# Experts' blocks of 96 rows for one expert and 32 rows for it or for a small guest expert

## The chip, the core and the metric

The kernel runs on one core of a Trainium2 chip. The metric is the device time of one execution in microseconds (us). The engines are TensorE (PE; its weight loads are listed apart as PEld), VectorE (DVE), ScalarE (ACT), GpSimd (POOL) and SyncE (SP).

## The reference

Two transformer blocks run one after the other over 512 tokens of width 1024, all in float32. The change lies in the end of the second one, a mixture of experts:

```
scores = sigmoid(h @ router_w); choice = scores + router_bias      # 512 x 64
# the 4 best of 8 groups of experts, in them the 8 best experts of each token
gw = scores of the 8, divided by their sum, times 2.5
y = sum over a token's 8 experts of gw * (silu(h @ gate_e) * (h @ up_e)) @ down_e
shared = (silu(h @ sh_gate) * (h @ sh_up)) @ sh_down
x = x + g2 * (y + shared)
out = rms_norm(x) * final_g
```

An expert's gate and up weights are 1024 x 256 each, its down weights 256 x 1024. There are 512 x 8 = 4096 pairs of token and expert. How many of them an expert gets is known only on the chip, from the router.

## The kernel before

The program is a list of phases. Each is a block in which every engine has its own instruction list, and semaphores order the lists. Three phases are touched.

**phase_route** computes the router's choice, then a plan. DVE runs a chain of small dependent steps (`step`, each waits for the one before). The plan cuts each expert's tokens into blocks of up to 128 rows, deals the blocks over lanes, and finds each token's slot. PE meanwhile computes the shared expert in the order of its list: `gate_up(0..3)`, counts and ranks, its down product, then `list_products`, which turns slots into lists of tokens. ACT copies the shared expert's result to `K.shared`.

**phase_experts** runs N trips. A trip has three steps s = 0, 1, 2 (UNROLL), each a block of 128 rows. Steps 0 and 1 use lanes 0 and 1, whose weights serve all 128 rows. Step 2 is split in halves of 64 rows, lanes 2 and 3, each with an expert and weights of its own (`halves`). N is the number of trips that holds all full blocks in lanes 0 and 1 and all halves. For each block

- POOL gathers the tokens' rows (`gather`) and loads the lane's weights (`load`), both by indirect DMA. A gate and up set is 2 MB and a down set 1 MB. A lane's weights are skipped where its expert is that of the trip before. Waiting for the buffers' last reader orders the loads: there is one buffer per lane, and it may be filled again when that lane's products of the trip before are done.
- DVE transposes the rows in 16 instructions (`move_x`).
- PE computes gate and up into a PSUM bank: 8 slices of the width, in each one `matmul` of the 128 tokens (or two of 64) against 512 columns. Then it computes the block before's down product (`down_products`, 4 pairs of slice and half), and two transposes of this block's product.
- ACT and DVE compute silu, the product and the copies out, and SP writes 512 KB to `expert_out`.

A float32 `matmul` instruction appears in the trace as two weight loads and two matmul records. In PE's rows a form like 128*64 is the shape of the weights, rows by columns of the array, and a tile of 64 columns writes 64 partitions of PSUM.

**phase_combine** gathers each token's 8 rows, sums 3 of them on DVE (on top of `K.shared`) and 5 on PE, and applies the gate, the residual and the last norm.

Of the kernel before, what the change touches and what calls it, by code (L numbers as in the profile page):

```python
# [13 lines left out]
P = 128  # L14
D = 1024
KD = D // P
T = 512
# [2439 lines left out]
LANES, LANE = 4, 32  # L2457
NOWHERE = 1.0e6
RC_LOWER, RC_TOKEN, RC_LANE, RC_TRIP, RC_ROW, RC_TWOS, RC_EXPERT, RC_COUNT, RC_N = 0, 64, 68, 69, 70, 71, 103, 167, 295


def phase_route(nc, K, ctx):
    d, sb, sig = K.dram, K.buffer, K.flag
    w_r, bias, const, tri = K.route_in
    K.shared = sb("shared", [P, NT, D])
# [4 lines left out]
    K.source = sb("lane_sources", [P, LANES * LANE]).bitcast(U32)  # L2470
    sc, tmp = (sb(n, [P, NT, EXPERTS]) for n in ("r_score", "r_tmp"))
    eq = sb("r_eq", [P, TOP, EXPERTS])
# [4 lines left out]
    full, fend, half, hend, hat, base, jump, got, got2 = (sb(f"r_{n}", [P, EXPERTS]) for n in ("full", "fend", "half", "hend", "hat", "base", "jump", "got", "got2"))  # L2477
    few, few_end, many = (sb(f"r_{n}", [P, EXPERTS]) for n in ("few", "few_end", "many"))
    ones = sb("r_ones", [P, EXPERTS])
    trips, num = sb("r_trips", [P, 2, LANE]), sb("r_num", [P, 24])  # L2480
    diag, again, src_f = sb("r_diag", [P, P]), sb("r_again", [P, P]), sb("r_src", [P, P])
# [9 lines left out]
    selected, cnt_mm, eb_done, eb_t = (sig(n) for n in ("selected", "counts_summed", "block_experts", "block_experts_turned"))  # L2491
    slots_done, hot, list_mm = sig("slots_ready"), sig("slot_digits_ready"), sig("lists_summed")
    gu_mm, sg_act, sh_mul, dn_mm, sh_out = (sig(n) for n in ("shared_gu", "shared_silu", "shared_product", "shared_down", "shared_out"))
    grp = lambda ap: ap.rearrange("p t (g e) -> p (t g) e", e=EXPERTS // GROUPS)
# [3 lines left out]
    with nc.Block() as block:  # L2498
        @block.sync
        def _(sp):  # L2500
            pass

        @block.tensor
        def _(pe):
# [20 lines left out]
            gate_up(2)  # L2525
            gate_up(3)
            pe.wait_ge(eb_done.sem, 1)
            eb_t.by(pe.matmul(K.bank[3][:, 0:P], K.ones[:, :], diag[:, :], start=True, stop=True))
            free(K, gu_mm)

            w = take(K, pe)[:, 0:2 * D].rearrange("p (k n) -> p k n", k=2)
# [20 lines left out]
        @block.scalar  # L2552
        def _(act):
            expo.by(act.activation(sc[:, :, :], K.psum[:, :].rearrange("p (t n) -> p t n", t=NT)[:, :, 0:EXPERTS], ACT.Exp, scale=-1.0))
            for m in range(2):
                act.wait_ge(gu_mm.sem, m + 1)
                sg_act.by(act.activation(hg[:, m, :], K.bank[4 + m], ACT.Silu))
            for n in range(2 * NT):
                t, half = divmod(n, 2)
                act.wait_ge(dn_mm.sem, n + 1)  # L2560
                sh_out.by(act.activation(K.shared[:, t, 512 * half:512 * half + 512], K.bank[6 + n % 2], ACT.Copy))

        @block.gpsimd
        def _(pool):
            pass

        @block.vector
        def _(dve):
# [47 lines left out]
            N, N2, F, F4, S = (num[:, m:m + 1] for m in range(5))  # L2616
            step(ts(full[:, :], cnt, BLOCK // 2 + 0.5, None, ALU.is_gt))
            step(ts(half[:, :], cnt, 0.5, None, ALU.is_gt))
            for k in range(1, T // BLOCK):
                step(stt(out=full[:, :], in0=cnt, scalar=BLOCK * k + BLOCK // 2 + 0.5, in1=full[:, :], op0=ALU.is_gt, op1=ALU.add))  # L2620
                step(stt(out=half[:, :], in0=cnt, scalar=BLOCK * k + 0.5, in1=half[:, :], op0=ALU.is_gt, op1=ALU.add))
            scan(fend, full)
            scan(hend, half)
            step(ts(trips[:, 0, :], const[:, RC_TWOS:RC_TWOS + LANE], fend[:, last:], None, ALU.is_lt))
            step(ts(num[:, 5:6], hend[:, last:], 0.5, None, ALU.mult))
            step(ts(trips[:, 1, :], const[:, RC_TWOS:RC_TWOS + LANE], num[:, 5:6], None, ALU.is_lt))
            step(tt(trips[:, 0, :], trips[:, 0, :], trips[:, 1, :], ALU.max))
            step(dve.tensor_reduce(N, trips[:, 0, :], AX.X, ALU.add))
            step(ts(N2, N, 2.0, None, ALU.mult))

            step(tt(half[:, :], half[:, :], full[:, :], ALU.subtract))
            step(stt(out=few[:, :], in0=full[:, :], scalar=0.5, in1=half[:, :], op0=ALU.is_lt, op1=ALU.mult))
            step(tt(many[:, :], half[:, :], few[:, :], ALU.subtract))
            scan(few_end, few)
            scan(hend, many)
            step(stt(out=hat[:, :], in0=hend[:, :], scalar=few_end[:, last:], in1=many[:, :], op0=ALU.add, op1=ALU.subtract))
            step(stt(out=got[:, :], in0=hat[:, :], scalar=N2, in1=many[:, :], op0=ALU.is_ge, op1=ALU.mult))
            step(tt(full[:, :], full[:, :], got[:, :], ALU.add))
            step(tt(many[:, :], many[:, :], got[:, :], ALU.subtract))
            scan(fend, full)  # L2640
            step(tt(hat[:, :], hat[:, :], many[:, :], ALU.mult))
            step(tt(few_end[:, :], few_end[:, :], few[:, :], ALU.subtract))
            step(tt(few_end[:, :], few_end[:, :], few[:, :], ALU.mult))
            step(tt(hat[:, :], hat[:, :], few_end[:, :], ALU.add))
            step(tt(half[:, :], few[:, :], many[:, :], ALU.add))
            step(stt(out=num[:, 6:7], in0=N, scalar=-4.0, in1=fend[:, last:], op0=ALU.mult, op1=ALU.add))
            step(ts(got[:, :], hat[:, :], N2, num[:, 6:7], ALU.is_ge, ALU.mult))
            step(stt(out=hat[:, :], in0=hat[:, :], scalar=N2, in1=got[:, :], op0=ALU.add, op1=ALU.add))
            step(tt(base[:, :], fend[:, :], full[:, :], ALU.subtract))
            step(stt(out=jump[:, :], in0=hat[:, :], scalar=1.0, in1=fend[:, :], op0=ALU.mult, op1=ALU.subtract))  # L2650
            step(tt(jump[:, :], jump[:, :], half[:, :], ALU.mult))

            V = num[:, 7:8]
            step(ts(num[:, 8:9], const[:, RC_TRIP:RC_TRIP + 1], N, NOWHERE, ALU.is_ge, ALU.mult))
            step(ts(V, const[:, RC_LANE:RC_LANE + 1], N, const[:, RC_TRIP:RC_TRIP + 1], ALU.mult, ALU.add))
            step(tt(V, V, num[:, 8:9], ALU.add))
            step(ts(got[:, :], base[:, :], V, None, ALU.is_le))
            step(stt(out=got[:, :], in0=fend[:, :], scalar=V, in1=got[:, :], op0=ALU.is_gt, op1=ALU.mult))
            step(stt(out=got2[:, :], in0=hat[:, :], scalar=V, in1=half[:, :], op0=ALU.is_equal, op1=ALU.mult))
            step(tt(got[:, :], got[:, :], got2[:, :], ALU.add))  # L2660
# [3 lines left out]
            link(dve, ts(diag[:, :], K.ident[:, :], num[:, 9:10], None, ALU.mult), eb_done)  # L2664

# [535 lines left out]
```

## Time and profile before

| what | us |
|---|---|
| median of 3 runs (2342.84 to 2349.06) | 2344.48 |
| span of the profiled execution, which is also its time | 2343.3 |
| phase_route (1606 to 1666) | 60.0 |
| phase_experts until PE's first product (1666 to 1681.7) | 15.7 |
| PE's first to last product of phase_experts (1681.7 to 2265.2) | 583.5 |
| rest, phase_combine (2265.2 to 2343.3) | 78.1 |

The span counts from the first to the last instruction. The last rows of the table add up to the stretch from 1606 us on. What comes ahead of that is the same program before and after.

### The profile page before, as it was taken

The numbers are of one execution on the slowest core, as the hardware profiler recorded it, in microseconds if no ns is written. First come the engines' busy times: TensorE is split into PE (matmuls) and PEld (weight loads), VectorE is DVE, ScalarE is ACT, GpSimd is POOL, SyncE is SP. The second block draws the span as 40 slices with busy tenths as digits, with TensorE's granted clock in tenths as the row PEclk, the third lists the DMA queues.
The fourth block names the chain that finished last, engine by engine and source line by source line (L and its number), as shares of the span: only waits on it lengthen the run. The fifth ranks groups of instructions, "written<-read, shape, count | busy, mean of one in ns | idle before, by whom it ended". The sixth has DMA issues, their size and how long they took to land. (4 is left out here: it accounts for less than half of the span.)

```text
span 2343.3 us, 27600 instructions
## 1 busy us (share of the span) xinstructions
PE 2151.4 (92%) x10395; PEld 1246.3 (53%) x10395; DVE 1330.6 (57%) x2524; ACT 461.2 (20%) x916; POOL 396.7 (17%) x771
## 2 busy tenths in 40 slices
PE   6999989999999999999879999998699999999975
PEld 3444554777785458883443788445333333333322
DVE  3448863766672134434968333535766766767745
ACT  2013561121120011004235232011011111111111
POOL 0005000111000000000000000000444444444433
PEclk9999999999999999999989999998799999999988
DMA  9422000535524015981111100401499999898976
GB/s 389 180 81 81 36 1 20 233 144 216 215 81 179 36 72 229 391 306 54 37 57 58 51 3 4 177 36 54 180 372 397 425 353 421 344 407 357 413 281 252
DMA packets 68999, 446.60 MB, mean 191 GB/s; under 512 B 12276, under 2 KB 12932, under 8 KB 44066
## 3 DMA queue, kind: packets, MB, share of 16 engines
q0 software_dynamic: 36176, 254.42, 27.1%
q1 hardware_dynamic: 32722, 190.78, 21.0%
q8 instruction: 71, 1.16, 0.2%
q14 instruction: 30, 0.24, 0.0%
HBM read 416.27 MB, written 73.45 MB: 209 GB/s over the span
## 5 line engine op out<-in xcount | busy, mean ns | idle before, releaser
L965 PE MATMUL psum<-arena 128*128 128x256 f32 x1904 | 416.7, 381 | 2.1 <-PEq L1005 2.0
L2824 PE MATMUL psum<-arena 128*64 128x512 f32 (+1 forms) x1088 | 366.1, 600 | 38.9 <-DVE arena L2872 16.6
L965 PEld LDWEIGHTS psum<-arena 128*128 128x128 f32 x1904 | 361.4, 190 | 62.6 <-issue 14.0
L2872 DVE STREAM_TRANSPOSE arena<-arena 32x256 f32<-32x256 f32 x832 | 362.1, 435 | 15.8 <-DMA arena<-scratch_h,arena 4.1
L2824 PEld LDWEIGHTS psum<-arena 128*64 128x64 f32 (+1 forms) x1088 | 143.8, 165 | 226.6 <-issue 197.7
L2815 PE MATMUL psum<-arena 128*64 128x512 f32 (+1 forms) x544 | 186.2, 598 | 1.2 <-ACT arena L2850 1.2
L1067 PE MATMUL psum<-arena 128*128 128x512 f32 x352 | 151.8, 592 | 0.3 <-PEq L1091 0.3
L2815 PEld LDWEIGHTS psum<-arena 128*64 128x64 f32 (+1 forms) x544 | 68.5, 163 | 113.2 <-issue 111.8
L869 PE MATMUL psum<-arena 128*128 128x512 f32 x256 | 111.2, 593 | 2.3 <-DVE arena L2432 1.5
L1067 PEld LDWEIGHTS psum<-arena 128*128 128x128 f32 x352 | 66.6, 190 | 83.4 <-issue 83.4
L2878 DVE COPY arena<-psum 128x512 f32<-128x512 f32 x51 | 35.3, 692 | 132.7 <-PE psum L2815 132.7
L420 DVE SCALAR_TENSOR_TENSOR arena<-arena 128x512 f32<-128x512 f32 x120 | 94.8, 833 | 5.8 <-PEq L456 4.5
L2846 ACT ACTIVATE arena<-psum 128x256 f32<-128x256 f32 x51 | 19.6, 384 | 378.2 <-PE psum L2824 371.0
L869 PEld LDWEIGHTS psum<-arena 128*128 128x128 f32 x256 | 48.1, 190 | 61.2 <-issue 58.9
L1200 DVE SCALAR_TENSOR_TENSOR arena<-arena 128x511 f32<-128x511 f32 x88 | 69.3, 788 | 16.0 <-ACT arena L1164 13.6
L1164 ACT ACTIVATE arena<-arena 128x512 f32<-128x512 f32 x44 | 33.5, 807 | 215.9 <-DVE arena L984 215.9
L2922 POOL DMA_INDIRECT arena<-in_exp_down,arena x68 | 69.3, 1018 | 34.2 <-issue 34.2
L2922 POOL DMA_INDIRECT arena<-in_exp_gu,arena x68 | 69.2, 1017 | 32.8 <-issue 32.8
L1600 PE MATMUL psum<-arena 128*128 128x512 f32 x128 | 63.9, 628 | 10.8 <-ACT arena L1700 8.8
L972 DVE TENSOR_TENSOR arena<-arena,psum 128x512 f32<-128x512 f32 x34 | 23.3, 687 | 88.8 <-PE psum L965 88.8
L244 PE MATMUL psum<-arena 128*32 128x512 f32 x384 | 49.6, 637 | 25.6 <-DMA arena<-in_w_ada 25.6
L1352 DVE TENSOR_TENSOR arena<-psum,arena 128x1024 f32<-128x1024 f32 x4 | 4.9, 1225 | 115.7 <-PE psum L1067 115.7
(521 smaller groups left out, 2932.0 us busy)
## 6 DMA issues: line engine op xcount, KB each, us to landing
scratch_expert_out<-arena SPq DMA_DIRECT2D x18, 2048.0 KB, 19.9
scratch_expert_out<-arena SPq DMA_DIRECT2D x51, 512.0 KB, 9.9
arena<-in_w_ada SPq DMA_DIRECT2D x12, 2048.0 KB, 16.8
arena<-in_ada_w POOLq DMA_DIRECT2D x12, 2048.0 KB, 8.8
arena<-in_w_up SPq DMA_DIRECT2D x22, 1024.0 KB, 4.8
arena<-in_w_in SPq DMA_DIRECT2D x9, 2048.0 KB, 11.0
arena<-in_w_down SPq DMA_DIRECT2D x5, 2048.0 KB, 8.6
arena<-in_w_o SPq DMA_DIRECT2D x2, 2048.0 KB, 8.4
```

The lines of the kernel that those rows point to most:

```text
L244: last = pe.matmul(bank[32 * j:32 * j + 32, :], vec[:, k, :], w[:, 512 * k:512 * k + 512], start=(r == 0), stop=(r == 1))
L420: K.tap.by(dve.scalar_tensor_tensor(out=conv[:, k, :], in0=x, scalar=w, in1=conv[:, k, :], op0=ALU.mult, op1=ALU.add))
L869: last = pe.matmul(K.bank[2 * t + half], lhs[:, k, P * t:P * t + P], row(k)[:, 512 * half:512 * half + 512], start=(k == 0), stop=(k == pe ...
L965: last = pe.matmul(out, w[:, k, :], x[:, k, :], start=(k == 0), stop=(k == KH - 1))
L1067: out = pe.matmul(K.bank[2 * t + half], K.hmid[:, k, P * t:P * t + P], w[:, k % 4, 512 * half:512 * half + 512], start=(first and k == inn ...
L1200: link(dve, dve.scalar_tensor_tensor(out=c[:, to], in0=u[:, fr], scalar=taps[:, n, 4 * half + tap:4 * half + tap + 1], in1=c[:, to], op0=A ...
L1600: last = pe.matmul(K.bank[6 if m == 0 else 7], K.gw[:, m % 2, P * k:P * k + P], K.h[:, k, :], start=(k == 0), stop=(k == KD - 1))
L2815: last = pe.matmul(K.bank[5 + half][r, :], ht[:, b, P * k + r.start:P * k + r.stop], down[:, lane, D * k + 512 * half:D * k + 512 * half + ...
L2824: last = pe.matmul(K.bank[2 + s][r, :], xt[:, s, P * k + r.start:P * k + r.stop], gu[:, lane, 2 * E_FF * k:2 * E_FF * (k + 1)], start=(k = ...
L2872: last = dve.transpose(channels[c:c + 32, :, a:a + 32], tokens[a:a + 32, :, c:c + 32])
L2878: dve.tensor_copy(out[:, (s - 1) % U, 512:D], K.bank[6]).then_inc(out_dve.sem, 1)
L2922: pool.indirect_dma_start(to[:, lane, :], None, src, offset, bounds_check=EXPERTS * P - 1, oob_is_err=False).then_inc(landed_[lane].sem, 16)
```

## The change

The 128 rows of a block become 96 rows of the lane's expert and 32 rows (partitions 0 to 31) that belong to it or to a guest. All three lanes are alike. Each has two weight buffers, OWN and VISITOR. An expert with at most 32 tokens (`tiny`) is a guest in a block whose 32 rows its host does not need (`spare`). A guest that finds no room becomes a host (`alone`). N is now a third of the number of hosts' blocks. The plan, the slots and the lists follow. `K.table` holds for each block which buffer its 32 rows use, and PE reads it (`choice`).

PE's product over 128 rows is issued in three parts, `rows_of`: rows 32 to 63 and rows 64 to 127 with OWN, then rows 0 to 31 with the buffer picked by a register. The loop's buffers change too: the weights take 2 x 3 sets instead of 4, `e_h` is gone (the product is written over `g`), `ht` has one buffer, and the third buffer of gathered rows shares memory with the router's scores. It is cleared and filled only when DVE's last use of them (`weigh_step`) is done.

In phase_route the shared expert's down weights are multiplied by the gate row on POOL, and POOL adds the shared expert's result to the residual `K.res` there. phase_combine starts its sum with a multiplication instead.

```
+            def choice(i, s):
+                return pe.value_load(table[0:1, at(i, s)], min_val=OWN, max_val=VISITOR)
+            def rows_of(bank, left, weights, lane_pick, col, first, last_):
+                for r in (slice(GUEST, 2 * GUEST), slice(2 * GUEST, P)):
+                    pe.matmul(bank[r, :], left[:, r], weights[:, OWN, col:col + 512], start=first, stop=last_)
+                picked = weights[:, bass.ds(lane_pick, 1), col:col + 512].rearrange("p a n -> p (a n)")
+                return pe.matmul(bank[0:GUEST, :], left[:, 0:GUEST], picked, start=first, stop=last_)
...
                 for half in range(2):
                     for k in range(2):
-                        for r, lane in halves(b):
-                            last = pe.matmul(K.bank[5 + half][r, :], ht[:, b, P * k + r.start:P * k + r.stop],
-                                             down[:, lane, D * k + 512 * half:D * k + 512 * half + 512], start=(k == 0), stop=(k == 1))
+                        last = rows_of(K.bank[5 + half], ht[:, P * k:P * k + P], down[b], pick, D * k + 512 * half, k == 0, k == 1)
...
             def step(i, s):
+                if s == 0:
+                    if not (isinstance(i, int) and i == 0):
+                        picks[U - 1] = choice(i, -1)
+                    picks[0] = choice(i, 0)
                 blocks_done(pe, turned, i, s, 0)
-                landed(pe, gu_in, i, s, 0)
+                landed(pe, gu_in, i, s, 0, 32)
                 for k in range(KD):
-                    for r, lane in halves(s):
-                        last = pe.matmul(K.bank[2 + s][r, :], xt[:, s, P * k + r.start:P * k + r.stop],
-                                         gu[:, lane, 2 * E_FF * k:2 * E_FF * (k + 1)], start=(k == 0), stop=(k == KD - 1))
+                    last = rows_of(K.bank[2 + s], xt[:, s, P * k:P * k + P], gu[s], picks[s], 2 * E_FF * k, k == 0, k == KD - 1)
                 last.then_inc(gu_mm.sem, 1)
                 if not (isinstance(i, int) and i + s == 0):
-                    down_products(i, s)
+                    down_products(i, s, picks[(s - 1) % U])
+                if s < U - 1:
+                    picks[s + 1] = choice(i, s + 1)
...
-                for _, lane in halves(s):
-                    offset = bass.IndirectOffsetOnAxis(ap=wrows[:, index + lane:index + lane + 1], axis=0)
-                    pool.indirect_dma_start(to[:, lane, :], None, src, offset, bounds_check=EXPERTS * P - 1, oob_is_err=False).then_inc(landed_[lane].sem, 16)
+                for who in (OWN, VISITOR):
+                    offset = bass.IndirectOffsetOnAxis(ap=wrows[:, index + 2 * s + who:index + 2 * s + who + 1], axis=0)
+                    pool.indirect_dma_start(to[s][:, who, :], None, src, offset, bounds_check=EXPERTS * P - 1, oob_is_err=False).then_inc(landed_[s].sem, 16)
...
-            link(pool, pool.memset(xg[:, :, :], 0.0), cleared)
+            link(pool, pool.memset(xg2[:, :, :], 0.0), cleared)
...
+                    if isinstance(i, int) and i == 0 and s == 1:
+                        pool.wait_ge(weigh_step.sem, 3 * NT)
+                        link(pool, pool.memset(xg[U - 1], 0.0), cleared)
```

Of the plan in phase_route (`parts` counts an expert's blocks, `own` those of them that need their 32 rows themselves):

```
+            step(stt(out=tiny[:, :], in0=cnt, scalar=GUEST + 0.5, in1=parts[:, :], op0=ALU.is_lt, op1=ALU.mult))
...
+            step(tt(host[:, :], parts[:, :], tiny[:, :], ALU.subtract))
...
+            step(tt(spare[:, :], host[:, :], own[:, :], ALU.subtract))
...
+            step(ts(trips[:, :], const[:, RC_THREES:RC_THREES + LANE], host_end[:, last:], None, ALU.is_lt))
+            step(dve.tensor_reduce(N, trips[:, :], AX.X, ALU.add))
...
+            for k in range(2):
+                gated.by(pool.tensor_tensor(shared_down[:, k, :], shared_down[:, k, :], gate_row[:, :], ALU.mult))
+            for t in range(NT):
+                pool.wait_ge(sh_out.sem, 2 * t + 2)
+                added.by(pool.tensor_tensor(K.res[:, t, :], K.res[:, t, :], shared[:, t, :], ALU.add))
```

**Where instructions move.** On PE, in the body of the loop, before: from step 0's down product to step 1's. L2824 is gate and up, L2815 down (here of the split lane, in 64-row parts), L2831 the transposes; the shape is that of the output.

```order
L2815 MATMUL psum<-arena 64x512 x8
L2831 MATMUL psum<-arena 128x128 x2
L2778 REGISTER_ALU
L2824 MATMUL psum<-arena 128x512 x8
L2815 MATMUL psum<-arena 128x512 x4
```

The same engine and place in the changed kernel, from the loop's first product on; L2834 and L2836 are the two kinds of line in `rows_of`, and this pattern of four rows stands 12 times in a block (8 in gate and up, 4 in down).

```order
L2811 ISA
L2820 ISA
L2834 MATMUL psum<-arena 32x512
L2834 MATMUL psum<-arena 64x512
L2836 ISA
L2836 MATMUL psum<-arena 32x512
L2834 MATMUL psum<-arena 32x512
L2834 MATMUL psum<-arena 64x512
```

Each instruction over 128 output rows has become three, of 32, 64 and 32 rows in that order, with a register instruction ahead of the third. On PE in the changed kernel, at the end of a block, between the down product and the transposes (L2868); L2830 reads the table for the next block.

```order
L2836 ISA
L2836 MATMUL psum<-arena 32x512
L2830 ISA
L2830 TENSOR_LOAD arena
L2830 ISA x2
L2868 MATMUL psum<-arena 128x128 x2
L2811 REGISTER_ALU
```

A read from memory into PE's registers now stands in each block. On POOL, in the loop's body, one step of lane 1 before (L2908 gathers rows, L2922 loads weights):

```order
L2908 DMA arena<-scratch_h,arena 128x1024
L2913 TENSOR_TENSOR arena<-arena 128x1
L2916 ISA
L2916 COPY arena<-arena 128x1
L2918 REGISTER_ALU
L2919 TENSOR_TENSOR arena<-arena 128x1
L2922 DMA arena<-in_exp_gu,arena 128x4096
L2913 TENSOR_TENSOR arena<-arena 128x1
L2916 COPY arena<-arena 128x1
L2919 TENSOR_TENSOR arena<-arena 128x1
L2922 DMA arena<-in_exp_down,arena 128x2048
```

The same step in the changed kernel (L2944 gathers, L2956 loads):

```order
L2944 DMA arena<-scratch_h,arena 128x1024
L2949 TENSOR_TENSOR arena<-arena 128x1
L2951 ISA
L2951 COPY arena<-arena 128x1
L2951 ISA
L2951 COPY arena<-arena 128x1
L2952 REGISTER_ALU
L2953 TENSOR_TENSOR arena<-arena 128x1
L2956 DMA arena<-in_exp_gu,arena 128x4096 x2
L2949 TENSOR_TENSOR arena<-arena 128x1
L2951 COPY arena<-arena 128x1 x2
L2953 TENSOR_TENSOR arena<-arena 128x1
```

Two loads of each kind are issued for every block, where lanes 0 and 1 issued one.

## Rows read from the trace of the kernel before

**Rows 1.** The page's part 1: busy us, share of the span, instructions.

```profile
PE 2151.4 (92%) x10395; PEld 1246.3 (53%) x10395; DVE 1330.6 (57%) x2524; ACT 461.2 (20%) x916; POOL 396.7 (17%) x771
```

**Rows 2.** Windows by stage: length, engines' busy us (count), granted clock, DMA share, GB/s.

```profile
core 0: us, PE busy (x) PEld busy (x) DVE busy (x) ACT busy (x) POOL busy (x), PEclk, DMA share, GB/s
...
1681.70:2265.20 583.50, 556.78 (x1734) 224.61 (x1734) 411.12 (x923) 63.52 (x152) 260.21 (x612) 0.99 0.94 381
2265.20:2343.30 78.10, 36.69 (x81) 15.43 (x80) 36.93 (x37) 13.62 (x37) 32.64 (x32) 0.78 0.66 262
...
1666.00:1681.70 15.70, 0.01 (x1) 0.01 (x1) 11.14 (x23) 0.00 (x0) 11.92 (x22) 0.63 0.54 202
```

**Rows 3.** Groups by form, 1700 to 2240 us: gate and up, whole and split.

```profile
L2824 PE MATMUL psum<-arena 128*128 128x512 f32 x510 | 226.0, 596 | 9.8 <-DMA arena<-in_exp_gu,arena 9.8
L2824 PE MATMUL psum<-arena 128*64 128x512 f32 x512 | 113.4, 595 | 12.6 <-issue 12.6
```

**Rows 4.** Window of one whole block of lane 0, PE: busy (count), clock, DMA, GB/s.

```profile
1867.08:1877.60 10.52, 10.52 (x28) 1.00 1.03 435
```

**Rows 5.** The transposes, by source line: min/median/max ns, first and last start.

```profile
L2831 PE MATMUL psum<-arena x102: 272/273/477, 1694.6 to 2260.1; 128*128 128x128 f32 x102
```

**Rows 6.** Timeline of PE's weight loads into, along and out of a split lane's products.

```profile
start us, us, engine line op out<-in xcount [idle before <-releaser]
...
1862.27 0.19 PEld L2824 LDWEIGHTS psum<-arena 128*128 128x128 f32 x1 [0.24 <-issue]
1863.22 0.20 PEld L2815 LDWEIGHTS psum<-arena 128*64 128x64 f32 x4 [0.76 <-issue]
1863.70 0.14 PEld L2815 LDWEIGHTS psum<-arena 128*64 128x64 f32 x2 [0.29 <-issue]
1864.13 0.14 PEld L2815 LDWEIGHTS psum<-arena 128*64 128x64 f32 x2 [0.29 <-issue]
...
1865.85 0.14 PEld L2815 LDWEIGHTS psum<-arena 128*64 128x64 f32 x2 [0.28 <-issue]
1866.81 0.20 PEld L2831 LDWEIGHTS psum<-arena 128*128 128x128 f32 x2 [0.81 <-issue]
1866.97 0.30 PEld L2824 LDWEIGHTS psum<-arena 128*128 128x128 f32 x2
```

**Rows 7.** Timeline of PE in an earlier phase, where three forms follow each other.

```profile
1128.43 0.61 PE L1630 MATMUL psum<-arena 128*128 128x128 f32 x4
1128.96 0.44 PE L1643 MATMUL psum<-arena 128*64 128x128 f32 x4
1129.33 0.49 PE L1618 MATMUL psum<-arena 64*128 64x256 f32 x2
```

**Rows 8.** Timeline of PE's weight loads, four tiles of 32 columns, first phase.

```profile
21.91 0.16 PEld L244 LDWEIGHTS psum<-arena 128*32 128x32 f32 x8 [2.90 <-DMA arena<-in_w_ada]
22.36 0.13 PEld L244 LDWEIGHTS psum<-arena 128*32 128x32 f32 x4 [0.30 <-issue]
22.79 0.13 PEld L244 LDWEIGHTS psum<-arena 128*32 128x32 f32 x4 [0.30 <-issue]
```

**Rows 9.** DMA, 1681.7 to 2265.2 us: all packets, and the indirect DMAs' queue.

```profile
DMA packets 33896, 222.39 MB, mean 381 GB/s; under 512 B 8841, under 2 KB 8841, under 8 KB 19264
...
q0 software_dynamic: 26691, 196.10, 82.7%
```

**Rows 10.** Reads of the table into registers, by source line: min/median/max ns.

```profile
L2762 PEldq TENSOR_LOAD <-arena x1: 487/487/487, 1666.1 to 1666.1; - x1
...
L2762 PEldq FUSED_REGOPS  x1: 175/175/175, 1666.6 to 1666.6; - x1
```

**Rows 11.** Timeline of DVE in the plan: two of its dependent steps.

```profile
1624.46 0.23 DVE L2620 SCALAR_TENSOR_TENSOR arena<-psum,arena 128x64 f32<-128x64 f32 x1
1624.72 0.22 DVE L2621 SCALAR_TENSOR_TENSOR arena<-psum,arena 128x64 f32<-128x64 f32 x1
```

**Rows 12.** POOL's groups by form: a sum of 128x1024, and the clearing in phase_experts.

```profile
L1270 POOL TENSOR_TENSOR arena<-arena 128x1024 f32<-128x1024 f32 x4 | 9.5, 2374 | 46.0 <-PE psum L965 46.0
...
L2928 POOL MEMSET arena<- 128x3072 f32 x1 | 2.7, 2657 | 199.6 <-POOLq L2498 199.6
```

**Rows 13.** What PE waited for, 1665 to 2270 us: us in total, times, longest.

```profile
PE psum L2824 <- DMA arena<-in_exp_gu,arena: 9.8, 10, 1.5
```

More of the change, by code:

```diff
@@ L2500, in _ @@
         def _(sp):
-            pass
+            gate_in.by(sp.dma_start(gate_row[:, :], d["mod_rows"][3].partition_broadcast(P)), 16)
         @block.tensor
@@ L2615, in _ @@
             last = EXPERTS - 1
-            N, N2, F, F4, S = (num[:, m:m + 1] for m in range(5))
-            step(ts(full[:, :], cnt, BLOCK // 2 + 0.5, None, ALU.is_gt))
-            step(ts(half[:, :], cnt, 0.5, None, ALU.is_gt))
+            N, F, G, V, AFTER, FREE, TURN, TURN1 = (num[:, m:m + 1] for m in (0, 1, 2, 7, 8, 15, 16, 17))
+            step(ts(parts[:, :], cnt, 0.5, None, ALU.is_gt))
             for k in range(1, T // BLOCK):
-                step(stt(out=full[:, :], in0=cnt, scalar=BLOCK * k + BLOCK // 2 + 0.5, in1=full[:, :], op0=ALU.is_gt, op1=ALU.add))
-                step(stt(out=half[:, :], in0=cnt, scalar=BLOCK * k + 0.5, in1=half[:, :], op0=ALU.is_gt, op1=ALU.add))
@@ L2622, in _ @@
[L2622 to L2651, printed above, removed]
@@ new lines, in _ @@
+            step(ts(own[:, :], got[:, :], 0.5, None, ALU.is_gt))
+            for k in range(1, T // BLOCK):
+                step(stt(out=own[:, :], in0=got[:, :], scalar=GUEST * k + 0.5, in1=own[:, :], op0=ALU.is_gt, op1=ALU.add))
+            step(tt(spare[:, :], host[:, :], own[:, :], ALU.subtract))
+            step(dve.tensor_reduce(F, spare[:, :], AX.X, ALU.add))
+            step(ts(F, F, -0.5, 1.0, ALU.mult, ALU.add))
+            step(stt(out=F, in0=tiny_end[:, last:], scalar=0.5, in1=F, op0=ALU.mult, op1=ALU.add))
@@ new lines, in _ @@
+            step(stt(out=alone[:, :], in0=tiny_end[:, :], scalar=F, in1=tiny[:, :], op0=ALU.is_lt, op1=ALU.mult))
+            step(tt(guest[:, :], tiny[:, :], alone[:, :], ALU.subtract))
+            step(tt(host[:, :], host[:, :], alone[:, :], ALU.add))
+            scan(host_end, host)
+            step(tt(base[:, :], host_end[:, :], host[:, :], ALU.subtract))
+            step(tt(start[:, :], base[:, :], own[:, :], ALU.add))
+            step(ts(trips[:, :], const[:, RC_THREES:RC_THREES + LANE], host_end[:, last:], None, ALU.is_lt))
@@ L2659, in _ @@
-            step(stt(out=got2[:, :], in0=hat[:, :], scalar=V, in1=half[:, :], op0=ALU.is_equal, op1=ALU.mult))
-            step(tt(got[:, :], got[:, :], got2[:, :], ALU.add))
+            step(stt(out=got[:, :], in0=host_end[:, :], scalar=V, in1=got[:, :], op0=ALU.is_gt, op1=ALU.mult))
+            step(stt(out=got2[:, :], in0=start[:, :], scalar=V, in1=got[:, :], op0=ALU.is_le, op1=ALU.mult))
+            link(dve, dve.tensor_reduce(FREE, got2[:, :], AX.X, ALU.add), spare_done)
             step(tt(got[:, :], got[:, :], const[:, RC_EXPERT:RC_EXPERT + EXPERTS], ALU.mult))
@@ L2740, in phase_experts @@
     U = UNROLL
[L2741 to L2744 removed]
+    OWN, VISITOR = 0, 1
+    gu, down = [], []
+    for lane in range(U):
+        gu.append(sb(f"e_gu{lane}", [P, 2, KD * 2 * E_FF]))
+        down.append(sb(f"e_down{lane}", [P, 2, 2 * D]))
+    xt, out = sb("e_xt", [P, U, D]), sb("e_out", [P, U, D])
+    g, ht, xg2 = sb("e_g", [P, U, E_FF]), sb("e_ht", [P, E_FF]), sb("e_x", [P, 2, D])
+    xg = [xg2[:, 0, :], xg2[:, 1, :], K.weigh[:, :]]
+    rows, wrows = sb("e_rows", [P, 8]).bitcast(U32), sb("e_weight_rows", [P, 4 * U]).bitcast(U32)
     wait_for = sb("e_wait_for", [P, 8])
@@ L2993, in _ @@
             for t in range(NT):
-                x, s = K.res[:, t, :], K.shared[:, t, :]
+                x, s = K.res[:, t, :], total[:, t, :]
                 for j in range(ON_DVE):
```

185 lines of the change are left out of this document (107 added, 78 removed).

## The prediction

> **What bounds the kernel now.** I read the page's busy times first, then the windows by stage, then PE's groups and loads in the loop. PE is busy for 92% of the span [rows 1]. The change touches the last 737 us, and of them the loop of phase_experts is 583.5 us long, with PE busy for 556.8 of it at granted clock 0.99 and the DMA engines for 94% [rows 2]. So two things are nearly full there. To see which one sets the pace, take one block: a whole-lane block takes 10.52 us with PE busy throughout [rows 4], which is 24 records of 0.43 us and two transposes. The transposes of the 51 blocks (102 records, two each) run from 1694.6 to 2260.1 us, so a block takes 11.3 us on average [rows 5]. The difference is half-speed clock and waits at the start, the changes of form in split blocks, and waits for weights (9.8 us in total that the profile names, [rows 13]). PE is the bound, with weight traffic close behind it.
>
> One more thing has to be read from the rows, the side-by-side work of narrow tiles. Of gate and up, 510 whole records take 226.0 us and 512 records of 64 columns 113.4 us [rows 3]: 0.443 and 0.221 us each. Two tiles of 64 columns share the array at full speed. Four tiles of 32 columns do so too: their loads come in fours, 0.43 us apart [rows 8].
>
> **What the change is meant to remove.** I worked out the router's choice from the reference's inputs and put the counts through both plans. Before: 29 full blocks and 39 halves, 17 trips, 51 blocks, which the 102 transposes confirm [rows 5], and 58 weight sets of 3.15 MB. These and 16.8 MB of gathered rows make 199 MB, of which 196.1 MB fall into the loop's window [rows 9]. After: 68 blocks, of which 22 are small enough to be guests and all find room; 46 hosts, so 16 trips, 48 blocks, 53 weight sets. Three blocks and five sets fewer. At 11.44 us a block (583.5 over 51) that would save 34 us, if a block kept its cost.
>
> **What a block costs then.** Every slice is now three tiles of 32, 64 and 32 columns in that order, two records each. They sit on different columns, so the best case is that all three run side by side. No row of the trace shows tiles of 32 and 64 columns next to each other, so the cost must be bounded from what a change of form costs elsewhere.
>
> In one form, the next record's weights load while the current one streams, into the very same columns: loads come every 0.43 us [rows 6]. At the change from 128 to 64 columns this stops. The last 128-column load is at 1862.27; its record streams from 1862.70 to 1863.13; the narrow loads come only at 1863.22, 0.09 us after the array is empty, and the second pair of records 0.48 us after the first instead of 0.43. On the way out it is the same: last load 1865.85, its record ends at 1866.71, the next form's load at 1866.81 [rows 6]. In an earlier phase 128x128, 128x64 and 64x128 follow each other. Four records of 0.107 us from 1128.43 end at 1128.86, and the next form starts at 1128.96, again 0.10 later [rows 7]. Since sharing columns does not delay a load within a form, it is the change of form that does: the array runs empty, 0.09 to 0.10 us pass, and the first weights load unhidden (0.05 us for 64 columns, and by the first step of [rows 8], 0.45 instead of 0.43, 0.02 for 32). I take this to hold for 32 against 64 columns as well, and this is the choice on which the forecast rests.
>
> The Trainium skill, page TensorEngine Tiling (Array Packing), section Key Properties, says that changing the tiling mode, not just the tile, drains the engine. By that rule each three-part product pays two such changes; the trace agrees where it holds a change of form (0.09 to 0.10 us, [rows 6, 7]), and no run yet shows it for tiles on separate columns. With the rule the sum is the 2990 us below, without it the 2325 us of the first rival.
>
> So follow PE's list. The third part of a slice (32 columns) and the first part of the next (32) are neighbours of one form, and run side by side; the 64-column part stands alone. In a block with its 8 + 4 slices that makes 13 phases of 32 columns and 12 of 64, each two records long. A 64 phase is 0.48 + 0.43 + 0.09 = 1.00 us, a 32 phase 0.45 + 0.43 + 0.10 = 0.98 us. 12 x 1.00 + 13 x 0.98 = 24.7 us; the transposes with one more change of form 0.4 us (1866.81 to 1867.08 plus 0.10, [rows 6]). A block is 25.1 us instead of 10.52, and 48 blocks 1205 us.
>
> Smaller terms. The start: before, the first transposes come 12.9 us after the first product (1681.7 to 1694.6, [rows 2, 5]), where 16 records of 0.43 us take 6.9, at a clock of 0.63 ahead of the loop [rows 2]. That is +6; with more records in that stretch I take +10. The register reads: each is 0.49 + 0.18 us [rows 10], one per block and one more per trip, 64 in all. If PE's sequencer is far enough ahead they cost nothing; if it never is, 43 us. I take 10, near the low end, because a block now leaves 8 us of down product ahead of each read. The register instruction ahead of every third part lies under a record of 0.43 us: 0. POOL issues four weight loads for every block now, and PE waits for both landings of a pair (32 for 16). Two sets, 6.3 MB, take 14.5 us at the 435 GB/s of a busy block [rows 4] and have most of a trip of 75 us to land in: 0. If blocks stayed at 11 us this cover would be thin; that is priced in the first rival. Behind POOL's new wait for `weigh_step` stand the third gather and step 1's loads, some 2 us later than before, and the third block starts 25 us after the first instead of 11: 0.
>
> phase_route: DVE has 10 more dependent steps of 0.26 us [rows 11], and five of them are wide ones at up to twice that: +4 us on a chain that PE's lists wait for. POOL's two gate products come before PE can do the shared down product, but the weights and the row are there long before, and its last sum, 2.4 us after the last copy [rows 12], lies beside the list products. Without that cover +3. The clearing is 2048 wide instead of 3072 of 2.66 us [rows 12]: -0.9. phase_combine has one multiplication for a multiply and add: 0, at best -2.
>
> Sum: 1205 + 10 + 10 - 583.5 = +641.5 for the loop, +3 around it. The profiled execution took 2343.3 us, 1.2 below the median of the three runs. 2343.3 + 645 = 2988, with the 1.2 some **2990 us**, 1.275 times. Without register reads and unhidden loads (0.95 us a phase) the likeliest case gives 2930; with all the reads and a little more per phase 3050.
>
> **Rivals.**
>
> First, on the other side: tiles of 32 and 64 columns on separate columns do not hold each other up. For it: within one form narrow tiles are free of each other [rows 3, 8], and the changes of form in the trace are all between shapes that overlap. [...] Against it: the delay at a change that columns do not explain [rows 6]. Then a block is 10.52 us and two changes of form, some 10.9, and 48 of them 522 us. What is left is waiting: two of 16 trips need five weight sets, five need four. A trip of five moves 18.4 MB, in 32.6 us of PE; at the 435 GB/s of a busy block it takes 42 [rows 4]. Between no such stall (2312) and every such trip at full price (2339): 2325 us. It decides below 583.5 / 48 = 12.2 us a block, that is, where a change of form costs under 0.06 us.
>
> Second, no pairing: the third part and the next first part do not run side by side, because a register instruction and an own access stand between the slices. Then 12 phases more of 0.86 us, 35.4 us a block, +495: 3485 us. Against it: tiles of equal form share the array although each instruction is two records in a row [rows 3, 8].
>
> Third, the clock: in the 25 us blocks only 64 of 128 columns work at a time, and if PE is granted the 1.2 GHz level for that, as it was for most of the idle stretch ahead of the loop (0.63 on average, [rows 2]), records take twice as long: 46 us a block, about 4000 us. Against it: in the loop PE never stands still for more than a tenth of a us in this case.
>
> Fourth, that the plan does not save a trip, for counts that differ on the chip: +25 us on the forecast, inside its range.
>
> **How the numbers follow.** The forecast 0.70, no pairing 0.10, low clock 0.03, free tiles 0.17. The range reaches from just under the likeliest case's own 2930 to 3050, to most of the unpaired case: 2900 to 3480, which leaves out free tiles, low clock and little more, 0.2. A measurement of this kernel tells some 0.3% from no change, 7 us. Free tiles split into 0.12 faster, 0.04 same and 0.01 slower; all the rest is slower: 0.84.
>
> **What would show it.** Right: matmul records of 32 and 64 columns in the loop never overlap in time; the load of a 64-column part comes 0.09 us after the 32-column records' stream; a block takes 25 us; DMA share in the loop falls under 0.5, for 209 MB in 1220 us. Wrong: three tiles starting within 0.02 us of each other, blocks of 11 us, waits for `in_exp_gu` taking the place; or phases of 0.86 us without a gap. 48 blocks (96 transposes) and 53 sets should show either way.

## The result and the profile after

The changed kernel takes 2982.8 us (median of 4 runs, 2979.2 to 2985.2); the kernel before takes 2344.9 beside it. The ratio is 1.2712, with an interval of 1.2693 to 1.2731. The forecast was 2990. The profiled execution took 2984.55 us, its span is 2982.6.

The page of the changed kernel: busy us and share of the span, then the span in 40 slices of 74.6 us, in tenths; the changed part begins in the 22nd.

```profile
PE 2815.8 (94%) x12219; PEld 1237.1 (41%) x12220; DVE 1316.8 (44%) x2480; ACT 457.8 (15%) x907; POOL 467.9 (16%) x869
...
PE   7999899999999998799999699999999999999995
...
PEclk9999999999999999999998799999999999999998
DMA  7420034543218920210211363554444544454306
```

PE's share of the span rises from 92 to 94% and every other engine's falls [rows 1]; the DMA engines, nearly full before, are idle for half of the loop. The windows by stage show it in numbers (length, engines' busy us, clock, DMA share, GB/s): from the first counts to the token lists, to PE's first product, the loop's products, the rest.

```profile
1628.30:1679.30 51.00, 42.96 (x155) 25.81 (x154) 44.51 (x130) 4.78 (x8) 9.68 (x4) 0.87 0.00 0
1679.30:1699.50 20.20, 0.00 (x1) 0.03 (x1) 15.52 (x29) 0.00 (x0) 10.69 (x20) 0.55 0.67 261
1699.50:2912.60 1213.10, 1211.29 (x3552) 209.19 (x3552) 383.06 (x863) 59.79 (x143) 316.45 (x706) 1.00 0.45 167
2912.60:2982.60 70.00, 39.48 (x81) 16.56 (x80) 34.90 (x37) 13.62 (x37) 34.49 (x32) 0.80 0.74 293
```

The loop's last product ends at 2911.7, a little ahead of the third window's end: the loop takes 1212 us instead of 583.5 [rows 2], with PE at granted clock 1.00 and busy for all but 2 us of it. Why, the timeline of PE's products in mid-loop shows.

```profile
1960.63 0.62 PE L2836 MATMUL psum<-arena 128*32 x1
1960.63 0.62 PE L2834 MATMUL psum<-arena 128*32 128x512 f32 x1
1961.08 0.59 PE L2836 MATMUL psum<-arena 128*32 x1
1961.09 1.60 PE L2834 MATMUL psum<-arena 128*32 128x512 f32 x3
1962.61 0.62 PE L2836 MATMUL psum<-arena 128*32 x1
```

L2836 is the guest tile, L2834 the two own tiles. Records of one tile start 0.43 us apart but are listed some 0.6 us long, so the starts tell the order. The guest tile of one slice and the first own tile of the next start together at 1960.63. Their second records start at 1961.08 and 1961.09, and the row of three that begins there goes on with the two records of the 64-column tile. Only then, at 1962.61, comes the next pair. So 32 and 64 columns take turns: 1.98 us for each slice, where a whole slice took 0.86. The transposes, two a block, fix the block's length (count, min/median/max ns, first and last start):

```profile
L2868 PE MATMUL psum<-arena x96: 272/300/329, 1720.0 to 2902.5; 128*128 128x128 f32 x96
```

The first pair starts at 1719.95, the last at 2902.37 (its second record at 2902.5): 47 periods of 25.158 us, and not one of them differs by 0.05. Before it was 11.3 [rows 5].

### The profile page after: what moved, and what is told of

It reads as the page before. It is cut to its first block and busy times, and to the rows that moved or that the text cites. A ratio compares the mean times of both kernels' runs of the same rounds, so it can differ in the third digit from the quotient of the medians.

```text
span 2982.6 us, 32083 instructions
## 1 busy us (share of the span) xinstructions
PE 2815.8 (94%) x12219; PEld 1237.1 (41%) x12220; DVE 1316.8 (44%) x2480; ACT 457.8 (15%) x907; POOL 467.9 (16%) x869
## 2 busy tenths in 40 slices
DMA packets 76346, 429.99 MB, mean 144 GB/s; under 512 B 21155, under 2 KB 21811, under 8 KB 52689
## 5 line engine op out<-in xcount | busy, mean ns | idle before, releaser
L2834 PE MATMUL psum<-arena 128*32 128x512 f32 (+1 forms) x2304 | 1149.0, 612 | 21.2 <-DMA arena<-in_exp_gu,arena 20.4
L2836 PE MATMUL psum<-arena 128*32 x1152 | 603.0, 605 | 0.0
L2834 PEld LDWEIGHTS psum<-arena 128*32 128x32 f32 (+1 forms) x2304 | 189.3, 121 | 514.1 <-issue 513.0
L2909 DVE STREAM_TRANSPOSE arena<-arena 32x256 f32<-32x256 f32 x784 | 341.2, 435 | 19.2 <-DMA arena<-scratch_h,arena 9.1
L2836 PEld LDWEIGHTS psum<-arena 128*32 128x32 f32 x1152 | 79.2, 108 | 468.2 <-issue 468.2
L2920 DVE TENSOR_TENSOR arena<-arena,psum 128x256 f32<-128x256 f32 x48 | 20.2, 422 | 472.3 <-ACT arena L2883 472.3
L2949 POOL TENSOR_TENSOR arena<-arena 128x1 f32<-128x1 f32 x96 | 19.2, 200 | 721.4 <-PE psum L2836 720.1
L2956 POOL DMA_INDIRECT arena<-in_exp_down,arena x96 | 97.3, 1013 | 42.3 <-issue 42.3
L2956 POOL DMA_INDIRECT arena<-in_exp_gu,arena x96 | 97.0, 1011 | 42.0 <-issue 42.0
L2878 ACT ACTIVATE arena<-psum 128x512 f32<-128x512 f32 x48 | 28.7, 597 | 363.5 <-PE psum L2836 363.5
## 6 DMA issues: line engine op xcount, KB each, us to landing
arena<-in_w_ada SPq DMA_DIRECT2D x12, 2048.0 KB, 16.7
```

The costliest lines, as they stand in the source:

```text
L2834: pe.matmul(bank[r, :], left[:, r], weights[:, OWN, col:col + 512], start=first, stop=last_)
L2836: return pe.matmul(bank[0:GUEST, :], left[:, 0:GUEST], picked, start=first, stop=last_)
L2909: last = dve.transpose(channels[c:c + 32, :, a:a + 32], tokens[a:a + 32, :, c:c + 32])
L2956: pool.indirect_dma_start(to[s][:, who, :], None, src, offset, bounds_check=EXPERTS * P - 1, oob_is_err=False).then_inc(landed_[s].sem, 16)
```

## The experiments

**Four tiles of one width.** The own rows 32 to 127 become three tiles of 32 columns; nothing else changes.

```diff
-                for r in (slice(GUEST, 2 * GUEST), slice(2 * GUEST, P)):
+                for r in (slice(GUEST, 2 * GUEST), slice(2 * GUEST, 3 * GUEST), slice(3 * GUEST, P)):
```

> The 96 own rows of a slice are three tiles of 32 columns instead of one of 32 and one of 64; the guest tile, the register reads, the weight traffic, the planner and everything outside the loop stay as in the changed kernel. Theory A (the changes between 32- and 64-column tiles make the loss): one form everywhere, four tiles side by side, two records of 0.43 us a slice, so a block takes 10.5 to 11 us and 48 blocks some 520 us; with the rest of the changed kernel around it, 2310 to 2350 us, the spread being weight traffic that PE would now wait for (gu and down DMA waits of 10 to 50 us). Rival B (the guest tile, whose weights are addressed by a register, cannot run beside its neighbours): a second phase of 0.86 us for each of 12 slices, about 21 us a block, 2820 us. Rival C (something outside the products, for example the register reads or the landings of four weight loads, sets the 25 us): no change, 2983 us.

Measured: 2336.5 us (2335.4 to 2338.8), ratio to before 0.9971 (0.9959 to 0.9984). One more instruction a slice takes away 646 us. PE's timeline in mid-loop:

```profile
1899.46 0.60 PE L2834 MATMUL psum<-arena 128*32 128x512 f32 x3
1899.48 0.59 PE L2836 MATMUL psum<-arena 128*32 x1
1899.89 0.61 PE L2834 MATMUL psum<-arena 128*32 128x512 f32 x3
1899.91 0.59 PE L2836 MATMUL psum<-arena 128*32 x1
```

The transposes by source line, and what PE waited for:

```profile
L2868 PE MATMUL psum<-arena x96: 272/327/475, 1713.8 to 2262.0; 128*128 128x128 f32 x96
```

```profile
PE psum L2834 <- DMA arena<-in_exp_gu,arena: 47.4, 15, 20.1
```

Here four tiles start within 0.02 us of each other (the guest tile up to 0.33 later in other blocks, at the same pace), the guest tile with its register address among them, every 0.43 us. Of the 47 block periods 32 are within 0.05 us of 10.81, and all 47 together are 40 us above it. Some 27 of the 40 are the waits for weights after the first one of 20.1. Most of the rest lies in five stretches, 20.4 us together, in which PE is busy at granted clock 0.50, each right behind a wait. Theory A stands, B and C fall.

**The same three tiles, sorted by width.** In each product all 64-column parts come first, then the pairs of 32.

```diff
-                for r in (slice(GUEST, 2 * GUEST), slice(2 * GUEST, P)):
+                for r in (slice(GUEST, 2 * GUEST),):
...
+            def wide_of(bank, left, weights, col, first, last_):
+                pe.matmul(bank[2 * GUEST:P, :], left[:, 2 * GUEST:P], weights[:, OWN, col:col + 512], start=first, stop=last_)
...
+                for k in range(KD):
+                    wide_of(K.bank[2 + s], xt[:, s, P * k:P * k + P], gu[s], 2 * E_FF * k, k == 0, k == KD - 1)
                 for k in range(KD):
                     last = rows_of(K.bank[2 + s], xt[:, s, P * k:P * k + P], gu[s], picks[s], 2 * E_FF * k, k == 0, k == KD - 1)
```

The down product has the same loop of `wide_of` ahead of its own.

> Same three tiles a slice as the changed kernel, but in another order: in gate and up all eight 64-column parts first, then the eight pairs of 32 columns, and in the down product likewise four and four. 4 changes between forms a block are left of 24. Theory A has two prices, which this tells apart: the work that no longer overlaps (24 phases of 0.86 us in place of 12: 20.6 us a block) and the empty array at each change (24 times 0.1 us and the load behind it). With 4 changes left a block is 20.6 + 0.5 + 0.4 = 21.5 us, 48 of them 1032 instead of 1208, so 2805 us (2790 to 2825). If the empty array at the changes were most of the loss, and wide and narrow tiles of one group overlapped, a block would fall to 11 to 13 us, 2350 to 2450. Rival C (not the order of the products): 2983.

Measured: 2806.2 us. The periods are 21.506 us, all alike; PE's timeline around a down product:

```profile
1901.08 0.59 PE L2834 MATMUL psum<-arena 128*32 128x512 f32 x1
1901.09 0.59 PE L2842 MATMUL psum<-arena 128*32 x1
1901.61 3.65 PE L2838 MATMUL psum<-arena 128*64 128x512 f32 x8
1905.19 0.62 PE L2834 MATMUL psum<-arena 128*32 128x512 f32 x1
1905.19 0.62 PE L2842 MATMUL psum<-arena 128*32 x1
```

Now the price splits. A phase of two records is 0.858 us (eight pitches from 1706.50 to 1709.93 in the four-tile kernel are 3.43). A block of the changed kernel has 25 phases and 26 changes of form (the two at the transposes included), the sorted one 24 and 5, the four-tile one 12 and 2. From changed to sorted: 25.158 - 21.506 - 0.858 = 2.79 us for 21 changes, 0.133 each. From sorted to four tiles: 21.506 - 10.807 - 12 x 0.858 = 0.40 for 3 changes, 0.134 each. Of the 14.35 us a block that the changed kernel loses against four tiles, 13 x 0.858 = 11.15 are work that doesn't overlap and 24 x 0.133 = 3.2 are the changes. Sorting saves most of the small part. In this order the two widths meet at only three places a block, so the run gives the price of a change; that they don't run together is shown by the changed kernel's timeline and the four tiles.

**The split alone, in the kernel before.**

```diff
+    tiles = lambda s: [(slice(32, 64), s), (slice(64, P), s), (slice(0, 32), s)] if s < 2 else halves(s)
...
-                    for r, lane in halves(s):
+                    for r, lane in tiles(s):
```

`down_products` uses `tiles(b)` likewise.

> The kernel before, with one thing of the change in it: the products of the two whole lanes are issued as tiles of 32, 64 and 32 columns, all with the lane's own weights. No new planner, no guests, no register read on PE, the same weight traffic. Theory A: each of the 34 whole-lane blocks goes from 10.5 to 25.1 us, +496 us, about 2840 us (2810 to 2860). Rivals B and C (the register-addressed tile, the register reads, the landings, the plan): 2345, within 1%.

Measured: 2822.7 us. The periods repeat as 25.2, 16.3 and 20.8 us (both products split; lane 1's down product alone; gate and up alone): 62.3 a trip, where one of the kernel before without a wait takes 32.2. The prices above were not taken from this kernel and fit it: with 0.245 us for the transposes (10.807 less 12 phases and 2 changes), 17 phases and 11 changes make 16.29 and 21 phases and 19 changes 20.79. The time is 17 us less than expected, although a trip costs 30.0 more and not 29.2: the periods of before lie 29 us above their shortest in all, 9.8 of it named waits for weights [rows 13], and here they repeat without any. Plan, guests and registers have no part in the loss.

**The guest tile at a fixed address.**

```diff
-                picked = weights[:, bass.ds(lane_pick, 1), col:col + 512].rearrange("p a n -> p (a n)")
+                picked = weights[:, OWN, col:col + 512]
```

> The changed kernel with the guest tile's products always reading the lane's own weights, at a fixed address: no register in the address of any product (the reads of the table stay). This leaves the guests' own weights out of the result. Theory A (form changes alone): blocks stay at 25.16 us and the time at 2978 to 2988 us. Rival B (an address from a register holds the tile up or keeps it from running beside its neighbour): each of 12 slices loses a delay; the time falls by 20 us or more.

Measured: 2986.0 us; periods 25.158. An address from a register costs nothing here.

**No sums on POOL.** POOL's four `tensor_tensor` into `K.res` are left out.

> The changed kernel without POOL's four sums of the shared expert into the residual, so this leaves the shared expert out of the output. Theory D (a DVE instruction that starts while POOL's 128x1024 sum runs is held until it ends, and that is where some 8 us of the later start of the loop come from): the four steps of 128x1024 and eight times 128x96 on DVE take 13.8 us in all, as before, instead of 21.6, none of the 128x96 instructions takes over 0.4 us, the first product comes 6 to 8 us earlier measured from the counts, and the time is 2975 to 2978. Rival (DVE is held by something else in this stage, its own row buffer or PE's lists): the four steps still take 21 us, 2983.

Measured: 2978.0 us. First the changed kernel: DVE's 32 short list instructions by source line (min/median/max ns), POOL's four sums in the timeline, and one of the DVE instructions that met a sum. Then DVE's line (renumbered) without the sums.

```profile
L2751 DVE TENSOR_SCALAR arena<-arena x32: 316/325/2494, 1656.1 to 1676.1; 128x96 f32<-128x96 f32 x32
```

```profile
1656.49 2.42 POOL L2585 TENSOR_TENSOR arena<-arena 128x1024 f32<-128x1024 f32 x1 [39.14 <-ACT arena L2575]
1659.92 2.37 POOL L2585 TENSOR_TENSOR arena<-arena 128x1024 f32<-128x1024 f32 x1 [1.01 <-ACT arena L2575]
1663.36 2.54 POOL L2585 TENSOR_TENSOR arena<-arena 128x1024 f32<-128x1024 f32 x1 [1.07 <-ACT arena L2575]
1666.79 2.34 POOL L2585 TENSOR_TENSOR arena<-arena 128x1024 f32<-128x1024 f32 x1 [0.89 <-ACT arena L2575]
```

```profile
1656.61 2.37 DVE L2751 TENSOR_SCALAR arena<-arena 128x96 f32<-128x96 f32 x1
```

```profile
L2748 DVE TENSOR_SCALAR arena<-arena x32: 321/325/332, 1656.3 to 1668.1; 128x96 f32<-128x96 f32 x32
```

With the sums, four of the 32 instructions take 2.24 to 2.49 us, one for each sum, and each ends within 0.1 us of its sum's end; without them none takes more than 0.33. The four steps take 13.4 us instead of 21.6, and the lists are ready 6.0 us earlier (1673.3 for 1679.3). The Trainium skill, page SBUF — State Buffer, section Who interferes with whom, says that VectorE and GpSimd share a port pair as an exclusive lock: where a VectorE instruction runs in a 2-port mode, which it says tensor_scalar can enter, whoever issues first holds the pair for the whole instruction and the other blocks. By that rule the four instructions wait out their sums, and the trace agrees (0.33 to 2.49 us); in which mode they ran, no run here shows.

**What the four-tile kernel still waits for.** Every guest row number is out of bounds and every table entry 0.

```diff
-            step(ts(K.source[:, 1, :], guests, float(P), const[:, RC_ROW:RC_ROW + 1], ALU.mult, ALU.add))
-            step(ts(K.table[:, 0:BLOCKS], guests[0:1, :], 0.5 * NOWHERE, None, ALU.is_lt))
+            step(ts(K.source[:, 1, :], guests, 0.0, NOWHERE, ALU.mult, ALU.add))
+            step(ts(K.table[:, 0:BLOCKS], guests[0:1, :], -1.0, None, ALU.is_lt))
```

> The four-tile kernel with every guest row number out of bounds and every table entry 0, so that 22 of its 53 weight sets are not loaded (the loads are still issued), and the guest tiles read the lane's own weights. This leaves the guests' own weights out of the result. In the four-tile kernel 27 of 47 block periods are the floor of 10.8 us, and the 47 together are 40 us above it; the first product came 20.1 us after PE began to wait. Theory E (what is left of PE's waits is weight traffic): with 31 sets the periods fall to 10.8 nearly everywhere (excess under 8 us), the first wait shortens by some 5 us (one load of 2.1 MB less ahead of it), and the time is 2290 to 2300 us. Rival (the waits come from the number of DMA issues or from the gathers of rows): the excess stays above 25 us, 2320 to 2337.

Measured: 2298.9 us. PE's waits:

```profile
PE psum L2834 <- DMA arena<-in_exp_gu,arena: 19.9, 2, 15.5
```

The first wait is 15.5 instead of 20.1, and 46 of 47 periods are at 10.81 (the first, 16.7, holds the other 4.4 us of that wait). As many loads are issued as in the four-tile kernel, and POOL's gathers are the same, so 34 of the 40 us came with the bytes of the guests' weights. (At the floor are 32 periods of the four-tile kernel, not the 27 of the expectation.)

**The residual added by PE**, and the same **with a late guest** (the last two lines of the diff, in that run alone).

```diff
+                last = pe.matmul(K.bank[6 + n % 2], K.ident[:, :], K.res[:, t, 512 * half:512 * half + 512], start=False, stop=True)
...
-                sh_out.by(act.activation(shared[:, t, 512 * half:512 * half + 512], K.bank[6 + n % 2], ACT.Copy))
+                sh_out.by(act.activation(K.res[:, t, 512 * half:512 * half + 512], K.bank[6 + n % 2], ACT.Copy))
...
-            for t in range(NT):
-                pool.wait_ge(sh_out.sem, 2 * t + 2)
-                added.by(pool.tensor_tensor(K.res[:, t, :], K.res[:, t, :], shared[:, t, :], ALU.add))
...
-            step(ts(want[:, :], guest_end[:, :], -0.5, G, ALU.add, ALU.mult))
+            step(ts(want[:, :], guest_end[:, :], -0.25, G, ALU.add, ALU.mult))
```

> The four-tile kernel with the residual added to the shared expert by PE (one more product a half with the identity matrix, into the same bank; ACT copies the sum straight into the residual) instead of by POOL. Theory D (POOL's sums hold DVE): the four DVE steps take 13.8 us instead of 21.6, the lists come 6 to 8 us earlier, 2327 to 2332 us. PE's 8 more products, 16 records of 0.43 to 0.86 us, lie in time in which PE waits for DVE's lists. Rival: they delay the lists, which come behind them on PE, and eat the gain: 2335 to 2340.

> As four32_pe_sum, and the spread of the guests over the free blocks is moved by a quarter of a step (one constant), so that the first block has no guest and needs one weight set instead of two; counts and trips stay. If the first wait of 20 us is the landing of two sets of gate and up, it falls to some 15 us, and the time is 4 to 5 us under that of four32_pe_sum: 2322 to 2328. If the total of the weight traffic sets the pace from the first load on, the gain is given back in later waits: the same as four32_pe_sum within 2 us.

Measured: 2338.6 us (0.9977 of before, 0.9968 to 0.9987) and 2340.3 (0.9980, 0.9970 to 0.9990); both rivals hold. DVE's line and PE's list products with PE's sums:

```profile
L2749 DVE TENSOR_SCALAR arena<-arena x32: 322/325/330, 1656.8 to 1668.6; 128x96 f32<-128x96 f32 x32
...
L2551 PE MATMUL psum<-arena x64: 246/275/275, 1673.4 to 1680.4; 128*128 128x96 f32 x64
```

DVE is free, yet the lists start only at 1673.4, when PE has done 22.3 us of shared down products and sums (15.8 us without sums): the wait moved from DVE to PE's own list. And the late guest cuts the first wait from 20.1 to 15.5 us, but the gain goes again in the next blocks (periods of 17.9, 17.2 and 17.2 us):

```profile
PE psum L2832 <- DMA arena<-in_exp_gu,arena: 49.8, 18, 15.5
```

**The sums on DVE**, after its last list operand and ahead of its wait for PE.

```diff
+            for t in range(NT):
+                dve.wait_ge(sh_out.sem, 2 * t + 2)
+                added.by(tt(K.res[:, t, :], K.res[:, t, :], shared[:, t, :], ALU.add))
             dve.wait_ge(list_mm.sem, 1)
```

> The four-tile kernel with the four sums of the shared expert into the residual on DVE, after its last list operand and ahead of its wait for PE's lists, instead of on POOL; PE's work is that of the changed kernel. Theory D: the four DVE steps take 13.4 us instead of 21.6, the sums (1.2 us each) fill the 4.9 us in which DVE waits for PE's lists, the lists come 6 to 8 us earlier, and so does the end: 2328 to 2332 us where the four-tile kernel took 2336.5. Rival (the place of the sums does not matter, since PE's shared down product at half clock ends the phase anyway, or since the loop's weight traffic takes the earlier start back, as it did with the late guest): 2335 to 2340.

Measured: 2328.6 us (2326.5 to 2331.3), ratio to before 0.9941 (0.9927 to 0.9954): 0.6% under the kernel before, and under the four-tile kernel, whose interval lies above. DVE's sums and its reading of the lists:

```profile
1665.68 4.63 DVE L2756 TENSOR_TENSOR arena<-arena 128x1024 f32<-128x1024 f32 x4
1670.41 0.26 DVE L2759 TENSOR_SCALAR arena<-psum 128x96 uint32<-128x96 f32 x1
```

From the counts to the lists it takes 44.8 us instead of 51.0, and the sums fill the time in which DVE waited.

**A second trace of before.**

> The kernel before, unchanged, for a second trace. Two differences between the two traces lie where the change does nothing or little: the first counts of the routing come 4.4 us later (1628.3 for 1623.9 us), and in phase_combine DVE waits 7.4 us at the second group of 128 tokens in the trace of before, where no later trace shows such a wait. If both vary from run to run, the second trace has the counts somewhere between 1622 and 1630 us and the wait absent or of another size; if they belong to the kernel before, both stand as in the first trace within 0.5 us.

Measured: 2344.6 us. Its windows, cut as the four above:

```profile
1628.20:1669.50 41.30, 38.89 (x149) 22.15 (x148) 33.35 (x120) 4.78 (x8) 0.00 (x0) 0.96 0.00 1
1669.50:1685.90 16.40, 0.12 (x1) 0.12 (x1) 11.50 (x24) 0.00 (x0) 11.89 (x22) 0.64 0.52 195
1685.90:2272.00 586.10, 558.13 (x1734) 225.41 (x1734) 411.51 (x924) 64.02 (x153) 260.10 (x612) 0.99 0.93 379
2272.00:2342.80 70.80, 38.68 (x80) 16.39 (x80) 36.54 (x37) 13.17 (x37) 33.69 (x32) 0.78 0.73 289
```

The counts come at 1628.2, as in the changed kernel, and the rest takes 70.8 us instead of 78.1 [rows 2]. Both differences vary from run to run and are none of the change's. What held DVE for 7.4 us in the first trace stays open.

## Why the prediction was right

**The block.** Forecast 25.1 us, measured 25.158. The step on which it rested, that a change between 32 and 64 columns stalls PE although the columns differ, is shown by the timeline, by one width (10.81) and by the split in the kernel before; sorting (21.51) gives its price. The load that the prediction named as a sign is there too: the 32-column records that start at 1961.08 have streamed by 1961.51, and the next load, of 64 columns, comes 0.10 us later.

```profile
1961.61 0.19 PEld L2834 LDWEIGHTS psum<-arena 128*64 128x64 f32 x2 [0.84 <-issue]
```

Its sizes hold: the forecast's phases of 1.00 and 0.98 us are 0.858 and 0.12 to 0.14 for the change, against 0.133 measured. The Trainium skill's rule (TensorEngine Tiling (Array Packing), Key Properties), that a change of mode and not of tile drains the engine, is what this trace shows.

**The plan.** 48 blocks, as 96 transposes say, and 183.57 MB of indirect loads from the routing's end to the loop's, where it was 199.26: 15.7 MB less, five sets of 3.15. All DMA in that stretch is 208.3 MB at a share of 0.45, as forecast (209, under 0.5).

**Terms that were mis-sized.** The total fits better than its parts. Against the second trace of before (us):

| part | forecast | measured |
|---|---|---|
| counts to lists | +4 | 41.3 to 51.0: +9.7 |
| lists to first product | -0.9 (the clearing) | 16.4 to 20.2: +3.8 |
| products of the loop | 1225 | 1212 |
| rest, from the last product's end | 0 to -2 | 71.3 to 70.9: -0.4 |

- That POOL's last sum "lies beside the list products" and so costs nothing failed. POOL's sums do lie beside other work, but they hold DVE, whose operands those products need. It cost 6 to 8 us. DVE's longer chain, forecast as +4, took 3.6 (21.9 us from the counts to the end of DVE's second product of 128x512, where it was 18.3).
- That two weight sets "have most of a trip of 75 us to land in" failed for the first block, which has no trip ahead of it: 3.8 us. Without a second set there the four-tile kernel's first wait is 15.5 us instead of 20.1.
- The register reads were taken at 10 us and cost 0: blocks with two reads are as long as the others, in four-tile blocks of 10.81 too. The start was taken at +10: from the first product to the first transposes it took 20.5 us, where 8 slices in mid-block take 8 x 1.98 = 15.8 and a change, so +4. 47 x 25.158 + 20.5 ahead + 9.3 behind is 1212.

So the +10 around the loop and the -13 in it that were not forecast cancel, and that the total fits to 8 us is in part luck.

**The rivals.** Free tiles: between unlike widths no run shows them, and their time, 2325, is near what equal widths give, 2336.5 and, with the sums on DVE, 2328.6. No pairing: refuted, guest and own tile of 32 start together. Low clock: refuted, granted clock 1.00 with at most half of the columns at work. A plan that saves no trip: refuted, 48 blocks.

**Where the saving of three blocks and five sets went**, once the widths agree: 34 us were there at an unchanged cost a block. With four tiles the loop's products take 566.2 us where the second trace of before has 585.6, a gain of 19. Without waits three periods fewer would save 29 us (47 of 10.81 for 50 of 10.74 on average); but what the periods hold above that, mostly waits for weights, grows from 31 to 40 us, now that a block can need two sets. The start takes 13 of the gain back.

## What to carry to other kernels

Here tiles shared the array only where they had one width. Where widths are mixed, try first to cut the wide ones to the narrowest, which costs instructions and cost no time here, before thinking of their order. Work handed to an idle engine isn't free if it holds another; look for a slot in which the engine that waits would do it. And check the terms of a sum one by one against the trace even where the sum fits.

## What the hardware showed unexpectedly

A DVE instruction of 0.33 us that met a POOL sum of 128x1024 took up to 2.49 us. An early one, a DVE product of 128x256, took 2.55 instead of 0.42 beside POOL's gate products, and cost nothing, because DVE still waited 1.22 us for PE at the counts behind it. And a skipped indirect load isn't empty: the run without guest loads moved 69 MB less than the four-tile kernel, but had 5632 more packets under 512 bytes (26787 for 21155), 128 for each of its 44 skipped loads.
